# Two halves of a row-maximum product placed apart among the score blocks of an attention kernel

## The reference

```
def block(qblk):
    sc = jnp.einsum('bqkgd,bskd->bkgqs', qblk, k, preferred_element_type=jnp.float32) * scale
    p = jax.nn.softmax(sc, axis=-1).astype(v.dtype)
    return jnp.einsum('bkgqs,bskd->bqkgd', p, v)
...
out_a = _gqa_blocked(qa, ka, va)
out_b = _neighbourhood_attention(...)
mixed = concat(_rmsnorm(out_a), _rmsnorm(out_b)); h = h + mixed @ w_out[i]
h = h + conv-gated MLP(h); h = h + gate * (p[i] @ w_ple[i]); return _rmsnorm(h, final_norm)
```

## Time and profile before

| What | Value |
|---|---|
| Runs | 2089.92, 2090.98, 2092.71 us, median 2090.98 |
| Profiled execution, span from first to last instruction | 2085.4 us |
| TensorE busy | 2031.3 us, 97% of the span |
| VectorE, ScalarE, GpSimd busy | 1307.6, 822.4, 486.8 us |
| Phases of group A | 24, from 343.78 us to about 574 us of the span |
| Phases with 4 key blocks / with 8 | 8 / 16 |

### The profile page before, as it was taken

One profiled execution on the slowest core, in us unless ns is written; L12 is line 12 of the kernel. 1 busy time (PEld: TensorE's weight loads), 2 busy tenths in 40 slices (PEclk: granted clock), 3 DMA queues, 4 the chain that ended last, 5 costly groups with the idle time before them and its releaser, 6 DMA issues.

```text
span 2085.4 us, 28974 instructions
## 1 busy us (share of the span) xinstructions
PE 2031.3 (97%) x9990; PEld 1623.2 (78%) x9990; DVE 1307.6 (63%) x1761; ACT 822.4 (39%) x1361; POOL 486.8 (23%) x339
## 2 busy tenths in 40 slices
PE   7999999999989999999999999999999999999996
PEld 6778887655667788788888888888888888887885
DVE  6799834888767855886665566556653543434546
ACT  6222212444467811363443344334433433424223
POOL 4112203666721134111122112211200100102101
PEclk9999999999999999999999999999999999999998
DMA  5151667411089241212211121211156544341103
GB/s 186 66 162 70 203 177 199 81 45 45 18 173 196 67 171 61 91 36 66 70 49 62 65 69 47 65 65 65 45 197 236 186 141 158 129 150 32 41 31 121
DMA packets 83264, 215.79 MB, mean 103 GB/s; under 512 B 26624, under 2 KB 27008, under 8 KB 83200
## 3 DMA queue, kind: packets, MB, share of 16 engines
q1 hardware_dynamic: 82336, 213.85, 33.4%
q10 hardware_dynamic: 864, 1.13, 0.1%
HBM read 156.75 MB, written 58.20 MB: 103 GB/s over the span
## 4 chain that ended last, share of the span: by engine, by line
PE 76%; DVE 9%; issue 7%; ACT 2%; POOL 2%; DMA 2%; SPq 1%; ACTq 0%; POOLq 0%; DVEq 0%
PE ps L326 22%; PE ps L328 22%; PE ps L327 22%; DVE qstd L748 2%; PE ps L1291 2%; POOL key_sum L1147 1%; DVE qt L761 1%; PE ps L1237 1%; DMA raw<-in_w 1%; PE ps L1325 1%; PE ps L1245 1%; DMA KLB<-qkl 1%; PE ps L1301 1%; DVE WL L322 1%; PE ps L1209 1%
## 5 line engine op out<-in xcount | busy, mean ns | idle before, releaser
L326 PE MATMUL ps<-NH,WH 128*128 128x512 f32 x840 | 334.3, 398 | 19.5 <-DVE WL L731 9.6
L327 PE MATMUL ps<-NL,WH 128*128 128x512 f32 x840 | 331.0, 394 | 0.0
L328 PE MATMUL ps<-NH,WL 128*128 128x512 f32 x840 | 330.9, 394 | 0.0
L2477 DVE TENSOR_TENSOR NL<-raw,NH 128x1024 fp32r<-128x1024 f32 x66 | 82.3, 1247 | 197.6 <-ACT NH L2330 197.6
L326 PE MATMUL ps<-NL,NH 128*128 128x512 f32 x528 | 205.9, 390 | 0.2
L326 PEld LDWEIGHTS ps<-NH,WH 128*128 128x128 f32 x840 | 160.2, 191 | 58.3 <-DVE NL L725 10.7
L327 PE MATMUL ps<-NH 128*128 128x512 f32 x528 | 205.5, 389 | 0.0
L328 PE MATMUL ps<-NL 128*128 128x512 f32 x528 | 205.4, 389 | 0.0
L326 PE MATMUL ps<-NH,AH 128*128 128x512 f32 x528 | 205.4, 389 | 0.0
L327 PE MATMUL ps<-NL,AH 128*128 128x512 f32 x528 | 205.4, 389 | 0.0
L328 PE MATMUL ps<-NH,AL 128*128 128x512 f32 x528 | 205.4, 389 | 0.0
(11 more groups left out here) (253 smaller groups left out, 4105.9 us busy)
## 6 DMA issues: line engine op xcount, KB each, us to landing
raw<-in_w SPq DMA_DIRECT2D x102, 512.0 KB, 3.4
A_raw<-in_wu SPq DMA_DIRECT2D x84, 256.0 KB, 2.6
act<-ca SPq DMA_DIRECT2D x22, 768.0 KB, 3.3
NH<-act SPq DMA_DIRECT2D x66, 256.0 KB, 3.4
xst<-in_xT SPq DMA_DIRECT2D x24, 256.0 KB, 3.6
H<-in_xT SPq DMA_DIRECT2D x8, 768.0 KB, 8.9
H<-hT SPq DMA_DIRECT2D x8, 768.0 KB, 6.4
out_yT<-H SPq DMA_DIRECT2D x24, 256.0 KB, 2.1
```

The lines of the kernel that those rows point to most:

```text
L326: nc.tensor.matmul(out, wh, xh, start=first, stop=False, skip_group_check=onto)
L327: nc.tensor.matmul(out, wh, xl, start=False, stop=False, skip_group_check=onto)
L328: return nc.tensor.matmul(out, wl, xh, start=False, stop=last, skip_group_check=onto)
L2477: nc.vector.tensor_tensor(NL[:, 2 * s:2 * s + 2, cols(g)], raw[:, s, :].rearrange("p (a n) -> p a n", a=2), NH[:, 2 * s:2 * s + 2, cols(g) ...
```

## The change

The two products of a pass over 1024 keys are issued one at a time, with score products between them. A pass over 512 keys keeps its place, and so do the products of phases whose next unit has 512 keys (b = 2 and 5) and the last phase of all. What changes are the 16 phases b = 0, 1, 3, 4. Number of instructions, waits, banks and values are the same.

```
-            def max_pass(p, b, t):
+            def max_part(p, b, t, part):
...
-                for c0 in range(0, w, GT):
-                    mm = nc.tensor.matmul(ps[:, 2 * (t % 2) + c0 // GT, :], q, KH["A"][s][:, k0 + c0:k0 + c0 + GT].bitcast(F32R),
-                                          start=True, stop=True)
-                mm.then_inc(s_rdy, 1)
+                k = k0 + part * GT
+                mm = nc.tensor.matmul(ps[:, 2 * (t % 2) + part, :], q, KH["A"][s][:, k:k + GT].bitcast(F32R), start=True, stop=True)
+                if k + GT == k0 + w:
+                    mm.then_inc(s_rdy, 1)
...
+                parts = window("A", 4 * after[1])[1] // GT if after else 0
+
+                def between(turn):
+                    t, part = divmod(turn, 2)
+                    if parts == 2:
+                        max_part(*after, t, part)
+                    elif part == 0:
+                        another(t)
+
                 first_pass(p, b, 0)
                 first_pass(p, b, 1)
-                another(0)
+                between(0)
                 second_pass(p, b, 0)
+                between(1)
                 second_pass(p, b, 1)
-                another(1)
+                between(2)
                 for kb in range(2, n):
                     first_pass(p, b, kb)
                     second_pass(p, b, kb)
-                    if kb in (3, 5):
-                        another(kb // 2 + 1)
+                    if n == 4:
+                        between(2 * kb - 1)
+                        between(2 * kb)
+                    elif kb < 7:
+                        between(kb + 1)
                 if n == 4:
-                    another(3)
+                    between(7)
```

More of the change, by code:

```diff
@@ L1210, in scores_b, with max_pass @@
                 nc.tensor.matmul(out, Q2[s][:, at:at + P].bitcast(F32R), keys(KL["B"][s]), start=False, stop=True).then_inc(s_rdy, 1)
-            def max_pass(p, b, t):
+            def max_part(p, b, t, part):
                 s, g = divmod(b, 3)
                 k0, w = window("A", 4 * b)
[L1215 to L1219, removed]
-                q = QS["A"][s][:, g * GT + t * P:g * GT + (t + 1) * P].bitcast(F32R)
-                for c0 in range(0, w, GT):
-                    mm = nc.tensor.matmul(ps[:, 2 * (t % 2) + c0 // GT, :], q, KH["A"][s][:, k0 + c0:k0 + c0 + GT].bitcast(F32R),
-                                          start=True, stop=True)
-                mm.then_inc(s_rdy, 1)
+                if part == 0:
+                    if b % 3 == 0 and t == 0:
+                        pe.wait_ge(q_ld["A"][s], queries_landed("A", p))
+                        pe.wait_ge(k_ld["A"][s], keys_landed("A", p))
+                    if not (isinstance(p, int) and p == 0 and b == 0 and t < 2):
+                        pe.wait_ge(m_done, p * ITEMS + (4 * b + t - 1))
+                q = QS["A"][s][:, g * GT + t * P:g * GT + (t + 1) * P].bitcast(F32R)
+                k = k0 + part * GT
+                mm = nc.tensor.matmul(ps[:, 2 * (t % 2) + part, :], q, KH["A"][s][:, k:k + GT].bitcast(F32R), start=True, stop=True)
+                if k + GT == k0 + w:
+                    mm.then_inc(s_rdy, 1)
+            def max_pass(p, b, t):
+                for part in range(window("A", 4 * b)[1] // GT):
+                    max_part(p, b, t, part)
             def max_rows(p, b):
```

## The result

The changed kernel takes 2100.12 us (median of 6 runs, 2096.24 to 2102.42), the kernel before 2090.45 (6 runs). The ratio is 1.0051, with a 95% interval of 1.0039 to 1.0063: slower by 8 to 13 us. I had forecast 2097.2 and a range up to 2099.5. The side was right, the size too small.

What follows compares the result with a forecast made beforehand. TensorE is 97% busy, but both ways to a four-block phase's end begin at VectorE's second reduction. Four-block 5.7 plus eight-block 0.5 gave 6.2 us, on 2091.0 thus 2097.2 us, range 2093.8 to 2099.5.

Steps and rivals of the forecast that it cites:

- Nothing is added; S0 doesn't come earlier; M0b 0.48 late: Four-block phases: same work, S0's load still 0.38 us after M0a, M0b and the first reduction 0.48 late.
- M1b behind S2, second reduction 0.73 late, 0.85 with a squaring: Four-block phases: M1b follows S2, so the second reduction starts 2.57 us after M0a, 0.73 late, or 0.85 with a squaring.
- the row: Profile row for F2's weight load: a product whose wait ends late pays 0.11 us; keeps 6.2 against the rule's 5.4.
- What is behind it: End of four-block phases: `last_addition` and later reductions follow the second reduction, so `sums`, transposes and phase are 0.73 us later.
- worse than the sum: Rival: `last_addition` beside GpSimd takes 0.2 or 0.3 us longer in seven phases, or the clock falls: 2099, chance 0.05.
- The first phase, 0.2: First four-block phase, without `last_addition`: S0 moves up 0.24, M1b ends 0.5 later, 0.26 is taken up; put at 0.2 us.
- Eight-block phases, 0.5: All eight-block phases: 4 x 0.02 + 3 x 0.08 + 0.15 = 0.5 us, most behind VectorE's outputs.
- nearly gone: Eight-block phase behind a four-block one: length unchanged to 0.1 us, and the wait at M2 nearly vanishes.
- Later stages late by the same amount: After group A: group B's loads wait for the last S, so no DMA slack takes up the delay; 6.2 us passes on.
- Faster: Rival: single products fill the gaps at M2 and F2, winning 1.9 + 3.2 = 5 us, 2086; chance 0.07.
- The first reduction alone, 3.6 us: Rival: only the first reduction's 0.48 us delay counts per four-block phase, about 3.6 in all, 2094.8; chance 0.10.
- Nothing to see: Rival: the delay is taken up, by a shorter `last_addition` or slack in group B's loads, 2091 to 2094; chance 0.08.

Runs made afterwards that it cites:

- The two runs in which GpSimd waits behind a moved product: GpSimd's second addition in four-block phases waits for `last_addition`, added to the changed kernel (1.0022) and to one with only M0b moved (1.0020), ratios against the kernel before.
- 0.4 alone: New order only in eight-block phases, four-block phases in the old order, against the kernel before: ratio 1.0007; eight phases 0.4 us longer in all.
- M0b alone: Only M0b moved behind S0, only in four-block phases, against the kernel before: ratio 1.0053, seven phases longer by 8.4 us.
- the phase of 7.55 us above: One four-block phase with a squaring when only M0b is moved, against the kernel before (run ratio 1.0053); the other two with a squaring took 8.66.

## Why the prediction was right about the side and wrong about the size

*Nothing is added; S0 doesn't come earlier; M0b 0.48 late.* Right: S0's load at 0.37 and the first reduction at 1.15 us behind M0a.

*M1b behind S2, second reduction 0.73 late, 0.85 with a squaring.* Right: 3.52 against 2.77 us into the phase, 0.75 late, and with a squaring 3.62 against 2.75, 0.87. F2's load again starts with its product, which again takes 0.50 us (437.36), so the row was the right guide for M1b. Seven phases would make 5.6 us of this.

*What is behind it: "`sums` and the final transposes are both 0.73 late, and the four-block phase is 0.73 longer".* This is the step that failed. I let `last_addition` keep its 0.85 us when it was moved in time, so its stretching stood at nothing in the sum. It took 1.44, the phases were 1.35 longer, and seven of them 9.5 instead of 5.5 us. The mechanism stood among the rivals, as *worse than the sum*, with 0.2 or 0.3 in seven phases and a chance of 0.05; it is 0.6. The two runs in which GpSimd waits behind a moved product show this part go when only GpSimd's start is changed, with the reductions as late: 8.58 becomes 7.83 (0.59, and the 0.16 of before too), and 8.57 becomes 7.54.

The size could have been read from the trace before. There 14 of its 16 `last_addition` started while GpSimd was at an instruction, and its time was 0.69 to 1.81 us. In each of the 14 it ended 0.54 or 0.55 us behind GpSimd's: 432.83 + 1.29 = 434.12 and 433.81 + 0.85 = 434.66 in the phase of the earlier trace rows. This phase, an eight-block one, has one of the longest (VectorE, then GpSimd, kernel before):

```profile
393.39 1.80 DVE L1541 TENSOR_TENSOR key_sum<-key_sum,key_part 128x512 f32<-128x512 f32 x1
...
393.36 1.29 POOL L1147 TENSOR_TENSOR key_sum<-PT 128x512 f32<-128x512 f32 x1 [3.91 <-ACT PT L1408]
```

The ends are 394.65 and 395.19, 0.54 again. With that rule and the start of the second addition at 4.39 us into the phase, `last_addition` at 4.78 ends at 4.39 + 1.27 + 0.55 = 6.21, which is what came. The Trainium skill says it ("SBUF — State Buffer", Who interferes with whom): a VectorE instruction with two inputs in SBUF and a GpSimd instruction that reads SBUF share a read port, and the second to issue blocks until the first finishes. The rows agree with it, up to 0.14 us: 0.55 us behind GpSimd's end is less than the 0.69 that `last_addition` takes alone.

*The first phase, 0.2.* Too small: 0.43 at a granted clock of 1.00. With the four-block phases alone in the new order, the last reduction ends only 0.16 later (7.31 against 7.15 us into the phase). But M3 waits for the late second reduction, and the products with the values behind M3 start 0.51 later (5.76 against 5.25).

*Eight-block phases, 0.5.* 0.16 in the changed kernel, 0.4 alone. Right in size. The wait at M2 isn't "nearly gone" though: its load still waits 0.38 us for the first reduction, against 0.59, and starts 3.89 us into the phase as before.

*Later stages late by the same amount.* Right: the last phase starts at 575.06 instead of 563.27 us, 11.8 of the 12.4 us between the spans.

*The rivals.* Faster: the gaps at F were partly filled, 98 waits became 82, and it won nothing, because the end of the four-block phase hangs on `last_addition`, on VectorE. The first reduction alone, 3.6 us: no; M0b alone costs 8.4 by the same step. Nothing to see: no; `last_addition` at another time took longer, not shorter.

## What to carry to other kernels

Before an instruction is moved in time, look at what runs beside it, now and at its new place, on VectorE and GpSimd above all: the duration of an addition of two SBUF operands isn't its own there. A start 0.1 us behind that of the other engine's addition made `last_addition` 1.72 us long instead of 0.69. In a chain that ends a phase, put such an addition where the other engine is idle, or let the engine with slack wait. A product that completes a group (the b halves here) is worth its earliest place if another engine's chain hangs on it, whatever gaps TensorE has.

## What the runs showed of the hardware

A VectorE addition of two 128x512 fp32 operands from SBUF took 0.69 us alone. Started while GpSimd was at an instruction, it ended 0.54 to 0.56 us after that one's end, whatever its own start, in every case of these eleven traces but one: 0.85, 1.44, 1.72 and 1.80 us among others. The other way round, a GpSimd addition that started during `last_addition` ended 1.12 to 1.16 us after its end, and took 1.5 to 1.8 us instead of the 1.26 to 1.29 of one alone. The one case is the phase of 7.55 us above: started 0.01 us behind GpSimd's addition, VectorE went first, and GpSimd's addition took 1.83 us. VectorE's reductions, which read PSUM, weren't held: in the kernel before, those over 1024 columns took 1.21 us wholly beside a GpSimd instruction (median of 32) and 1.22 with GpSimd idle (9).

The granted clock fell to its lower level, 1.2 GHz, at 341 to 343 us in four of eleven profiled executions, just ahead of group A or at its start, after 198 us at the upper level in three of them and 273 in the fourth, in kernels of either order. The first phase was 0.75 us (7.95 against 7.20) to 1.76 us longer with it (9.39 against 7.63). It may be part of the spread between the runs of one kernel, and what brings it about stays open.
